# Sub-key scores one query tile later in the PEER stage of a diffusion layer kernel

## The reference

```python
q = (h @ w_query).reshape(t, PEER_HEADS, 2, PEER_KEY_DIM // 2)      # 8 heads x 2 halves of 128
scores = jnp.einsum('thpd,hpnd->thpn', q, sub_keys)                 # against 128 sub keys each
top_s, top_i = lax.top_k(scores, PEER_TOPK)                         # 16 best of 128
cand_s = top_s[:, :, 0, :, None] + top_s[:, :, 1, None, :]          # 16 x 16 sums
best_s, best_j = lax.top_k(cand_s.reshape(t, PEER_HEADS, 256), PEER_TOPK)
# then: softmax gates, u-rows of the chosen experts times h, gelu, v-rows weighted and summed
```

## Time and profile before

| | |
|---|---|
| runs before | 2205.62, 2203.00, 2203.11 us, median 2203.11 us |
| span of the profiled execution | 2198.6 us |
| PE busy | 2089.7 us, 95% |
| PEld busy | 1810.6 us, 82% |
| DVE busy | 1550.8 us, 71% |
| ACT busy | 813.1 us, 37% |
| POOL busy | 951.0 us, 43% |
| DMA | 471.59 MB, mean 214 GB/s |

### The profile page before, as it was taken

The page is one execution under the profiler, slowest core; times in us unless marked ns, Lnnn a source line. Parts: engine busy times, 40 slices in busy tenths (PEclk is TensorE's granted clock), DMA queues, the critical chain, the costliest instruction groups (busy, mean ns, idle before and its releaser), DMA issues.

```text
span 2198.6 us, 39922 instructions
## 1 busy us (share of the span) xinstructions
PE 2089.7 (95%) x13950; PEld 1810.6 (82%) x13950; DVE 1550.8 (71%) x3564; ACT 813.1 (37%) x1300; POOL 951.0 (43%) x583
## 2 busy tenths in 40 slices
PE   5899999999999998999999999999998999999997
PEld 2688888888767876888999999999996888888885
DVE  5777776777531117567989889988456988888888
ACT  3444443443323334333433333333342333333332
POOL 1323333322414446444798756656783222222221
PEclk9899999999999998999999999999999999999998
DMA  6222222222213345334688869989999999999993
GB/s 263 98 83 93 92 83 83 87 80 85 78 58 106 96 152 164 114 101 125 204 289 258 268 217 337 329 315 333 369 359 353 371 369 344 354 332 349 352 324 113
DMA packets 151785, 471.59 MB, mean 214 GB/s; under 512 B 15633, under 2 KB 46577, under 8 KB 148337
## 3 DMA queue, kind: packets, MB, share of 16 engines
q1 hardware_dynamic: 109936, 303.21, 40.5%
q0 software_dynamic: 36864, 134.23, 16.7%
q10 hardware_dynamic: 4864, 32.51, 3.7%
HBM read 416.89 MB, written 53.00 MB: 214 GB/s over the span
## 4 chain that ended last, share of the span: by engine, by line
PE 74%; DVE 10%; DMA 5%; POOL 4%; issue 3%; ACT 2%; SPq 1%; DVEq 0%; ACTq 0%; POOLq 0%
PE bank L2762 23%; PE bank L569 11%; PE bank L571 10%; PE bank L570 10%; DMA rows<-peer_u,e_row 3%; POOL w_lo L1205 3%; PE bank L2748 2%; PE bank L2363 1%; PE pair L569 1%; PE bank L2373 1%; PE bank L2566 1%; DVE rows L1963 1%; PE pair L571 1%; PE pair L570 1%; DMA gq<-g_dram 1%
## 5 line engine op out<-in xcount | busy, mean ns | idle before, releaser
L1205 POOL TENSOR_TENSOR w_lo<-raw,w_hi 128x1024 fp32r<-128x1024 f32 x148 | 360.0, 2434 | 556.4 <-ACT w_hi L774 289.1
L569 PE MATMUL bank<-lat_hi,w_hi 128*128 128x384 f32 (+1 forms) x1480 | 538.6, 364 | 8.4 <-DVE lat_lo L1890 4.6
L570 PE MATMUL bank<-lat_lo,w_hi 128*128 128x384 f32 (+1 forms) x1480 | 523.4, 354 | 0.0
L571 PE MATMUL bank<-lat_hi,w_lo 128*128 128x384 f32 (+1 forms) x1480 | 523.1, 353 | 0.0
L569 PEld LDWEIGHTS bank<-lat_hi,w_hi 128*128 128x128 f32 x1480 | 281.7, 190 | 24.1 <-issue 9.5
L1323 POOL DMA_INDIRECT rows<-peer_v,e_row x128 | 138.3, 1081 | 365.2 <-DVE pair L2104 340.3
L571 PEld LDWEIGHTS bank<-lat_hi,w_lo 128*128 128x128 f32 x1480 | 280.8, 190 | 18.7
L570 PEld LDWEIGHTS bank<-lat_lo,w_hi 128*128 128x128 f32 x1480 | 281.7, 190 | 14.1 <-issue 0.2
L2762 PE MATMUL bank<-w_hi,c_hi 128*128 128x512 f32 x768 | 241.6, 396 | 8.1 <-DVE w_lo L2092 8.1
L1205 POOL TENSOR_TENSOR w_lo<-raw_more,w_hi 128x1024 fp32r<-128x1024 f32 x80 | 196.8, 2462 | 119.5 <-ACT w_hi L998 66.7
L2762 PE MATMUL bank<-w_lo,c_hi 128*128 128x512 f32 x768 | 241.2, 395 | 0.0
(11 more groups left out here) (376 smaller groups left out, 3546.4 us busy)
## 6 DMA issues: line engine op xcount, KB each, us to landing
raw<-w SPq DMA_DIRECT2D x210, 512.0 KB
raw_more<-w SPq DMA_DIRECT2D x142, 512.0 KB
g_dram<-gs ACTq DMA_DIRECT2D x24, 1024.0 KB
gq<-g_dram SPq DMA_DIRECT2D x48, 512.0 KB
gu_dram<-gu SPq DMA_DIRECT2D x120, 192.0 KB
gl<-gu_dram SPq DMA_DIRECT2D x30, 768.0 KB
ada<-w_ada SPq DMA_DIRECT2D x32, 512.0 KB, 4.2
dY<-gc_dram SPq DMA_DIRECT2D x8, 768.0 KB, 4.2
```

The lines of the kernel that those rows point to most:

```text
L569: nc.tensor.matmul(out, hi, rh, start=start, stop=False)
L570: nc.tensor.matmul(out, hi, rl, start=False, stop=False)
L571: return nc.tensor.matmul(out, lo, rh, start=False, stop=stop)
L1205: nc.gpsimd.tensor_sub(w_lo[:, slot, :], raw_at(slot % 2 if src is None else src), w_hi[:, slot, :].bitcast(F32)).then_inc(split_done, 1)
```

## The change

The scores of tile s are issued after query tile s+1 in place of right after query tile s (for an odd s there was a u pass between, and there it now comes after that u pass and the next query tile), and those of tile 15 after the last u pass. ScalarE's copy of the scores of s moves from the end of round s to round s+1, between the copy of the query tile and the rounding of the weights. ScalarE's loop is written out.

```diff
+            def keep_scores(s):
+                act.wait_ge(tk, max(TK_N * (s - 1), 0))
+                act.wait_ge(s_mm, s + 1)
+                nc.scalar.copy(sc[:, s % 2, :, :].rearrange("p a b -> p (a b)"), bank[4 + s % 2][:, :]).then_inc(s_ev, 1)
+
-            with act.Fori(0, 2) as i:
+            for i in range(2):
                 for j in range(PH):
                     act.wait_ge(q_mm, i * PH + (j + 1))
                     nc.scalar.copy(qq[:, j % RING, :], bank[j % 2][:, :]).then_inc(q_ev, 1)
+                    if i + j:
+                        keep_scores(i * PH + j - 1)
                     hi_n(T_QUERY + RING + 3 * (j // 2) + j % 2, i, 12)
                     if j % 2:
                         act_u(i, 4, j // 2)
                         hi_n(T_QUERY + RING + 3 * (j // 2) + 2, i, 12)
-                    act.wait_ge(tk, i * (PH * TK_N) + max(TK_N * (j - 1), 0))
-                    act.wait_ge(s_mm, i * PH + (j + 1))
-                    nc.scalar.copy(sc[:, j % 2, :, :].rearrange("p a b -> p (a b)"), bank[4 + j % 2][:, :]).then_inc(s_ev, 1)
+            keep_scores(2 * PH - 1)
...
+            def score_set(s):
+                pe.wait_ge(q_ev, s + 1)
+                pe.wait_ge(s_ev, max(s - 1, 0))
+                if s == 0:
+                    pe.wait_ge(ld_late, 64)
+                for b in range(LAT):
+                    last = mm(bank[4 + s % 2][:, b * P:(b + 1) * P], qq[:, s % RING, b * P:(b + 1) * P],
+                              sk[:, s, :], start=True, stop=True)
+                last.then_inc(s_mm, 1)
...
                     last.then_inc(q_mm, 1)
+                    if i + j:
+                        score_set(i * PH + j - 1)
                     if j % 2:
                         pe.wait_ge(split_done, i * 12 + (T_QUERY + n + 2))
                         pe.wait_ge(gelu, i * 4 + max(j // 2 - 1, 0))
                         scores_u(j // 2, (n + 1) % RING)
-                    pe.wait_ge(q_ev, i * PH + (j + 1))
-                    pe.wait_ge(s_ev, i * PH + max(j - 1, 0))
-                    if j == 0:
-                        pe.wait_ge(ld_late, 64)
-                    for b in range(LAT):
-                        last = mm(bank[4 + j % 2][:, b * P:(b + 1) * P], qq[:, j % RING, b * P:(b + 1) * P],
-                                  sk[:, bass.ds(i * PH + j, 1), :].rearrange("p o n -> p (o n)"), start=True, stop=True)
-                    last.then_inc(s_mm, 1)
+            score_set(2 * PH - 1)
```

## The result

The changed kernel takes 2192.82 us (median of 8 runs, 2187.17 to 2203.68) against 2203.52 us (8 runs, 2196.59 to 2210.42) for the one before, ratio 0.9949, 95% interval 0.9934 to 0.9965: 7.7 to 14.5 us less, with 2190.9 forecast. The profiled execution is the slowest of its eight, 2203.68 us with a span of 2201.8. It is late before the change begins: the first query tile ends at 889.23 where it was 881.06, 8.17 us of the front end, which both kernels share. So the two traces are compared stage by stage and not by their spans.

A forecast was written before the change was run, and what follows sets the result against it. TensorE, with 74% of the chain of waits, was taken as the bound, idling ahead of score matmuls. 3.87 + 1.81 + 6.51 = 12.19 us, other parts zero, so 2203.1 - 12.2 = 2190.9 us, range 2187.0 to 2197.0.

The forecast's parts named there:

- Part 1: First score set: its sub-key wait and slow scores go, 3.87 us, and the next tile's low clock, 1.81 us.
- Part 2: Even score sets 2 to 14 no longer wait for ScalarE's `qq` copy: 7 x 0.93 = 6.51 us go.
- Sum on TensorE: From the first query tile's end to the long run of u passes: 142.22 us becomes 130.03, 12.19 less.
- Part 3: ScalarE's new place for the score copy delays weight rounding and splits; about 10 us of slack, so zero cost.
- Part 4: ScalarE's loop written out removes a second table load, 1.28 us, and the jump: zero gain.
- Part 5: After the query stage: VectorE's last top 16 gains 0.7 us less than TensorE, vanishing in its 2.30 us fetched-row wait.
- Rival 1: TensorE's full clock doesn't hold even without a pause: about 2.9 us lost, gain 9.3, 2193.8 us; chance 0.07.
- Rival 2: VectorE and fetches take part back at `eidx` pauses: gain 5 to 10, chance 0.14; or up to 15, chance 0.06.
- Rival 3: The load ahead of the v stage doesn't move, its pause grows: 2203 us; chance 0.07 together with rival 5.
- Rivals 4 and 5: Slow top 16 holds ScalarE's weights, 2221 us, chance 0.04; second tile waits for weights or bank, 2203, 0.07 with rival 3.

The follow-up runs named there:

- this part alone: The changed kernel, but only score set 0 is issued one query tile later, all other sets at their old place: 2198.40 us against 2204.18 for the kernel before.
- the filler kernel: The kernel before, with twelve extra matmuls with unused results behind the first query tile: 2201.85 us against 2204.18 for the kernel before.

## Why the prediction was right

- **Part 1, first set.** Right in mechanism, and in size for its trace: 5.66 us measured with this part alone against 3.87 + 1.81. What it left out is that the landing of the sub keys varies: pauses of 2.81, 2.75, 2.17 and 2.06 us in four traces, and a stage of 140.38 in the second trace of before. The term is worth 3.8 to 5.7 us (3.8 is 142.22 - 140.38 less than 5.66). That the clock follows from the pause was a condition of the sum; the filler kernel showed it.
- **Part 2, even sets.** 7.05 us measured, 6.51 forecast. Odd sets: nothing forecast, 0.28 us lost.
- **Sum on TensorE.** 12.43 us, forecast 12.19; the parts give the same, 5.66 + 7.05 - 0.28. The rest is small: tile 1 takes 5.53 us (889.23 to 894.76) and not 5.57, and the period of a pair is 16.92 and not 16.95, seven times.
- **Part 3.** No wait of TensorE for weights or for its banks; the old place within the round gives the same stage. The prediction is one set off: `keep_scores(s - 1)` waits for the top 16 of s-3 and not of s-2, which only adds slack.
- **Part 4.** Nothing in the stage, by the loop alone. The count was wrong: the loop has four table loads in this stage (880.20, 897.58, 953.08 and 969.10), written out it has one, so three are gone and not one. The 5.3 us of ScalarE that the prediction estimates for two switches from the page "ScalarE: Activation LUTs" of the Trainium skill (What ACT_TABLE_LOAD costs) stayed off the path. Nor does a trace show the drain of that page: the copy behind the load at 880.20 starts at 881.49, 0.01 us after its end.
- **Part 5, handing over.** The timeline of VectorE shows where it was imprecise:

```profile
1015.39 0.15 DVE L1928 COPY mark<-cst 128x1 f32<-128x1 f32 x1 [0.88 <-ACT sc L1097]
...
1022.50 0.15 DVE L1928 COPY mark<-cst 128x1 f32<-128x1 f32 x1
...
1090.56 1.22 DVE L1969 SCALAR_TENSOR_TENSOR rows<-rows,pair 128x1024 f32<-128x1024 f32 x1 [2.54 <-DMA rows<-peer_u,e_row]
```

The top 16 of set 14 took 7.1 us and not 5.87 (1015.39 to 1022.50), since one of its copies was drawn out (1.41 us). The last top 16 starts 3.48 us behind the run of u passes, before 1.42; the lag is 2.1 us, not 0.7. It vanished at the first fetched row all the same, where VectorE still waited 2.54 us. The first fetch of expert rows was issued at 1081.63, so at 1073.5 when the 8.17 us are taken off, forecast 1073.7.

- **Rivals.** Rival 1 is out (clock 1.00). Rival 2 named the right place, the pauses at the expert numbers, and the first trace shows 7.7 us there; the second trace of each kernel shows that 3.6 of it, the first pause, falls either way without the change; the rest, the third pause, stays open. Rival 3 is out: counted from the end of tile 0 the first v matmul came 7.1 us earlier in the first pair of traces and 12.6 in the second, and the pause behind it was 8.09 and 7.93 us against 8.10. Rivals 4 and 5 didn't occur.
- **The forecast time.** 12.2 us of gain, against 10.7 and 10.0 us in the two groups with the changed kernel, intervals 7.7 to 14.5 and 6.0 to 13.7. So the first lies in the band that the prediction called its forecast (10.5 to 14), near its lower edge, and the second just below it, beside that of rival 2 (5 to 10); the intervals reach into both. The shortfall of 1.5 to 2.2 us is inside both intervals. The varying sub-key load and the third pause are each about large enough to make it; neither is shown.

## What to carry to other kernels

An engine that waits for an eviction of its own last result loses more than the idle time that the trace shows: 0.68 us idle, 1.0 us lost for each even set. Where a pause also lets the clock fall, as that for the sub keys did, the matmuls behind it pay too. Independent work issued in between buys both back. Price such a change by the distance from start to start of each kind of block, with and without its wait, and compare traces stage by stage, since one trace's span can be 8 us off before the change begins. When a pause shows up longer behind the change, take a second trace of both kernels before you book it.

## What the runs showed of the hardware

- TensorE's granted clock fell to the 1.2 GHz level at a pause of 2.81 us, between stretches at 2.4 GHz (0.50 over the 5.7 us behind it), and twelve filler matmuls over the same 3 us kept it up. In the second trace of the kernel before it fell at 2.06 us (0.56 over the 3.9 us behind), and in that of the changed kernel it held through 2.60 us (1.00 over 6.8 us). Pauses of 0.68 us in every pair didn't touch it (1.00 over 102.9 us).
- VectorE's `pick` product of two tensors in on-chip memory, 128x2048 in fp32, and GpSimd's work held each other off. The product took 2.3 to 2.4 us with the way free and 7.1 to 7.5 us when GpSimd was ahead, through a fetch and two weight splits (2.7 to 5.6 us also occur); GpSimd's fetch was drawn out from 0.96 to 2.8 us in the other order. The page "GPSIMD Engine Reference" of the Trainium skill (Specifications) says that GpSimd's interfaces to this memory are shared with VectorE for VectorE instructions with two inputs there; these traces agree, and add that the product didn't get in between a fetch and a split of GpSimd, 0.02 us apart (1127.28 to 1127.30), nor between the two splits.
